# Turning raw input rows on TensorE and applying the RMS factor afterwards, in a hybrid decoder trunk

## The chip, the cores and the metric

The kernel runs on one core of a Trainium2 chip. The metric is the device time of one execution in microseconds (us), median of several runs. Before the change it is 637.72 us (3 runs, 635.66 to 637.82).

## The reference, cut to what matters

One inference step for 272 prompt rows (16 meta rows and 256) and 32 sample rows, 304 in all, of width 1024, in float32. Only its beginning is touched by the change:

```
xp = concatenate([meta, x_prompt])                 # 272 rows; x_sample gives 32 more
xn = x * rsqrt(mean(x * x, axis=-1) + EPS) * norm1_g
proj = xn @ w_in                                   # 1024 x 6144
u_x, u_y, c_v, c_g, g_rnn, g_conv = split(proj)
```

What follows: a gated recurrence on u_x (a convolution over 4 rows, block-diagonal gates, a linear scan), a convolution over 31 rows on c_v * sigmoid(c_g) with a layer norm, two projections, a gated merge, w_out and a residual, then a second RMS norm, a router that picks 2 of 32 experts for each row, the experts, and a last RMS norm.

## The kernel before, in words

Each engine has a program of its own, written out by hand in order; semaphores connect them. An engine does its instructions in that order, so an instruction that waits holds up all that stands behind it on the same engine.

**Layout.** The 304 rows arrive as three row tiles (`x[:, t]`, 128, 128 and 48 rows, rows on the partitions). The projections want channels on the partitions, so x is turned into `xnT`, eight column blocks of 128 channels by 304 rows. `w_in` comes in blocks of 512 columns (2 MB) through four slots of a buffer called `ring`. A tile of the projection is 128 output channels by 304 rows: eight matmuls into one PSUM bank (`bank[m % 4]`). The order of tiles is cv 0, cg 0, cv 1, cg 1 and so on, then ux, uy, gr, gc. After tile 2 TensorE turns the convolution's states (`conf_states`, line 1327).

**SyncE (lines 345 to 370)** issues x in five loads, the first half of weight block 0, nine small parameter loads of 4 KB (lines 355 and 357), then the weight blocks (line 367). Block 2 waits until all of x is turned, because the scaled rows `xn` lie in its slot; block 3 waits for the states' transposes.

**ScalarE (from line 530)** issues four larger parameter loads (the two convolutions' weights, two states), loads a function table, and squares the rows of x as they land, with a sum (line 550). It takes the root (line 553), later evicts every odd column block with the scale `norm1_g` (line 558), and then issues the convolution's state and the gates' weights (lines 560 to 568) before it comes to the projection's tiles.

**VectorE (from line 842)** finishes 1 / root (lines 854, 856), scales the rows (line 860), copies the turned parameters and states from PSUM (lines 863, 866), and evicts every even column block with `norm1_g` (line 871). Then it makes a few constants, copies the states (line 893), and goes on to the convolutions (lines 907, 910, 938).

**TensorE (from line 1312)** does 24 warm-up matmuls, waits for all 13 parameter loads (`par_in`), turns parameters (line 1319) and recurrence states (line 1322), waits for the scaled rows, turns them (line 1337, 8 column blocks of 3 transposes, through banks 4 to 7), waits for all evictions, and starts on tile 0 (line 1375).

Of the kernel before, what the change touches and what calls it, by code (L numbers as in the profile page):

```python
# [7 lines left out]
ALU = mybir.AluOpType  # L8
ACT = mybir.ActivationFunctionType
# [6 lines left out]
P = 128  # L16
HP = P // 2
D = 1024
KT = D // P
# [4 lines left out]
T = TP + NS * TS  # L24
ROWS = (P, P, T - 2 * P)
NT = len(ROWS)
# [23 lines left out]
BLOCK_WORDS = KT * WB  # L50
# [7 lines left out]
RESULTS_BEFORE = 2  # L58
ST_DMAS = 6 + NS
WO_BANKS = (0, 1, 2, 3, 6, 7)  # L60
TURN_BANKS = (4, 5, 4, 5, 4, 5, 3, 6)
EXP_WORDS = 2 * KT * F + FT * D

# [18 lines left out]
def trunk(nc, a, o):  # L82
    with ExitStack() as ctx:
# [3 lines left out]
        start = {}  # L87
# [12 lines left out]
        bank = [ctx.enter_context(nc.psum_tensor(f"bank{i}", [P, 512], F32))[:, :] for i in range(8)]  # L100


        ring = sb("ring", EXP_SLOTS * EXP_WORDS)
        x = sb("x", NT * D).rearrange("p (t d) -> p t d", t=NT)
        work = sb("work", WORK)
# [11 lines left out]
        def chan(ap):  # L117
# [4 lines left out]
        xnT = chan(cut(KT * T))  # L122
# [11 lines left out]
        at_glu, at_cc = KT * (T + UXN + HN), KT * (T + UXN + HN + GLN)  # L134
# [45 lines left out]
                for s in range(MIX_SLOTS)]  # L180
        w_hi = [rounded(f"w_hi{s}", "ring", e_hi + s * BLOCK_WORDS // 2, BLOCK_WORDS // 2) for s in range(HI_SLOTS)]

        xn = ring[:, 2 * BLOCK_WORDS:2 * BLOCK_WORDS + NT * D].rearrange("p (t d) -> p t d", t=NT)
        cut(0, 3 * BLOCK_WORDS)
        prow = cut(6 * P).rearrange("p (i n) -> p i n", i=6)
        crow = cut(16 * P).rearrange("p (i n) -> p i n", i=16)
# [21 lines left out]
        pn1, pccb, plg, plb, prcb, pba, pbi, plam = (par[:, i * KT:(i + 1) * KT] for i in range(8))  # L208
# [18 lines left out]
        ident, ones_d = sb("ident", P), sb("ones_d", P)  # L227
        tri, ones_b = sb("tri", P, BF16), sb("ones_b", P, BF16)
        lam = sb("lam", 5 * KT).rearrange("p (i c) -> p i c", i=5)
        stat, spare = sb("stat", 18), sb("spare", 1)  # L230


        (xhi_done, xlo_done, wlo_pool, par_in, first_in, cst_in, wbd_in, router_in, g_in, consts, zeros, dconst, dstep, astep, pstep, rstep,
         ss_done, ms_done, rs_done, xn_done, par_T, par_done, rst_T, rst_done, cst_T, cst_done, xT_done, xnT_done, xnT_act,
         lam_e, kappa_done, tile_mm, tile_act, tile_dve, glu_done, win_done, win_used, conv_done, xc_done,
         gate_mm, gate_act, dec_done, vsq_done, vrt_done, inp_done, scan_done, gelu_done, prod_done,
         st_cp, st_T, st_ev, st_out, mean_mm, cen_done, sq_done, sum_done, var_mm, var_done, std_done, nrm_done, silu_done,
# [3 lines left out]
         chi_done, clo_done, mhi_done, mlo_done, eg_mm, gu_mm, silu2, hid_done, dn_mm, ys_act, ys_dve,  # L241
         yT_mm, yT_act, yT_dve, y_mm, y_done, ss3_done, ms3_done, rs3_done, fin_done, y_out) = (sem(n) for n in (
            "xhi_done xlo_done wlo_pool par_in first_in cst_in wbd_in router_in g_in consts zeros dconst dstep astep pstep rstep "
            "ss_done ms_done rs_done xn_done par_T par_done rst_T rst_done cst_T cst_done xT_done xnT_done xnT_act "
            "lam_e kappa_done tile_mm tile_act tile_dve glu_done win_done win_used conv_done xc_done "
            "gate_mm gate_act dec_done vsq_done vrt_done inp_done scan_done gelu_done prod_done "
            "st_cp st_T st_ev st_out mean_mm cen_done sq_done sum_done var_mm var_done std_done nrm_done silu_done "
# [95 lines left out]
        def _(sp):  # L343
# [6 lines left out]

            sp.dma_start(mix_w[0][:, 0:HB], block_src(*blocks[0])[:, 0:HB]).then_inc(first_in, 16)

            for i, n in enumerate(("norm1_g", "conf_conv_b", "conf_ln_g", "conf_ln_b",
                                   "rnn_conv_b", "b_rg_a", "b_rg_i", "rg_lambda")):
                sp.dma_start(prow[i * KT:(i + 1) * KT, 0], a[n][0].rearrange("(c p) -> c p", p=P)).then_inc(par_in, 16)

            sp.dma_start(prow[64:64 + KT, 3], a["norm2_g"][0].rearrange("(c p) -> c p", p=P)).then_inc(par_in, 16)

            def load_block(b):
                if b == 2:  # L360
                    sp.wait_ge(xT_done, KT)
                if b == 3:
                    sp.wait_ge(cst_T, 4)
                if b >= MIX_SLOTS:
                    sp.wait_ge(*block_used(b - MIX_SLOTS))
                k = slice(HB if b == 0 else 0, KT)
                sp.dma_start(mix_w[b % MIX_SLOTS][:, k], block_src(*blocks[b])[:, k]).then_inc(mix_in[b % MIX_SLOTS], 16)
# [159 lines left out]
        @block.scalar  # L527
        def _(act):

            act.dma_start(prow[64:96, 0], a["rnn_conv_w"][0].rearrange("w (c p) -> (w c) p", p=P)).then_inc(par_in, 16)  # L530
            act.dma_start(prow[0:124, 1:3], a["conf_conv_w"][0].rearrange("w (c p) -> (w c) p", p=P)
                          .rearrange("(i r) p -> r i p", i=2)).then_inc(par_in, 16)
# [14 lines left out]
            act.wait_ge(dconst, 1)  # L547
            for t in range(NT):
                act.wait_ge(x_in[t], 16 if t == 1 else 32)
                nc.scalar.activation(xn[0:ROWS[t], t], x[0:ROWS[t], t], ACT.Square,  # L550
                                     accum_out=stat[0:ROWS[t], t:t + 1]).then_inc(ss_done, 1)
            act.wait_ge(ms_done, 1)
            nc.scalar.activation(stat[:, 3:6], stat[:, 3:6], ACT.Sqrt).then_inc(rs_done, 1)

            act.wait_ge(par_done, 1)
            for j in range(1, KT, 2):
                act.wait_ge(xT_done, j + 1)
                nc.scalar.activation(xnT[:, j], bank[4 + j % 4][:, 0:T], ACT.Copy, scale=pn1[:, j:j + 1]).then_inc(xnT_act, 1)  # L558

            act.dma_start(crow[0:120], a["state_conformer_conv"][0].rearrange("s r (c p) -> (s r c) p", p=P)  # L560
                          .rearrange("(i q) p -> q i p", i=16)).then_inc(cst_in, 16)
# [6 lines left out]
            act.dma_start(o["cc_s"][0][:, 0:CW - 1 - TS], a["state_conformer_conv"][0][:, TS:]).then_inc(st_out, 16)  # L568


            nc.scalar.activation(lam[:, 0], plam, ACT.Abs).then_inc(astep, 1)
            act.wait_ge(astep, 1)
            nc.scalar.activation(lam[:, 0], lam[:, 0], ACT.Exp, scale=-1.0).then_inc(lam_e, 1)
# [256 lines left out]
        def _(dve):  # L830
# [20 lines left out]
            def inverse_root(i, done, ms, rs):  # L851

                dve.wait_ge(done, NT)
                vec.tensor_scalar(stat[:, i + 3:i + 6], stat[:, i:i + 3], 1.0 / D, EPS, ALU.mult, ALU.add).then_inc(ms, 1)
                dve.wait_ge(rs, 1)
                step(vec.reciprocal(stat[:, i + 3:i + 6], stat[:, i + 3:i + 6]))

            inverse_root(0, ss_done, ms_done, rs_done)
            for t in range(NT):
                vec.tensor_scalar(xn[0:ROWS[t], t], x[0:ROWS[t], t], stat[0:ROWS[t], 3 + t:4 + t], None,  # L860
                                  ALU.mult).then_inc(xn_done, 1)
            dve.wait_ge(par_T, 1)
            vec.tensor_copy(par, bank[0][:, 0:416]).then_inc(par_done, 1)

            dve.wait_ge(rst_T, 1)
            vec.tensor_copy(state_cols(ux, UXP, UXS)[:, :, 0:RW - 1],
                            bank[1][:, 0:192].rearrange("p (s r c) -> p s r c", s=NS, r=RW - 1)).then_inc(rst_done, 1)
            dve.wait_ge(par_done, 1)
            for j in range(0, KT, 2):
                dve.wait_ge(xT_done, j + 1)  # L870
                vec.tensor_scalar(xnT[:, j], bank[4 + j % 4][:, 0:T], pn1[:, j:j + 1], None, ALU.mult).then_inc(xnT_done, 1)

            dve.wait_ge(lam_e, 1)
            e, z, z2, q = lam[:, 0], lam[:, 3], lam[:, 4], lam[:, 1]
# [431 lines left out]
        def _(pe):  # L1306
# [21 lines left out]
                ins.then_inc(cst_T, 1)  # L1328


            pe.wait_ge(xn_done, NT)
            for j in range(KT):
                if j >= 4:
                    pe.wait_ge(xnT_done if j % 2 == 0 else xnT_act, (j - 4) // 2 + 1)
                for t in range(NT):
                    n = ROWS[t]
                    ins = tp(bank[4 + j % 4][:, t * P:t * P + n], xn[0:n, t, j * P:(j + 1) * P], ident[0:n, 0:n])
                ins.then_inc(xT_done, 1)
            pe.wait_ge(par_done, 1)
            pe.wait_ge(rst_done, 1)  # L1340
            pe.wait_ge(xnT_done, KT // 2)
            pe.wait_ge(xnT_act, KT // 2)

            def tile(m):
                k, c = tiles[m]
                b = blocks.index((k, c // MB))
                if m == 0:
                    pe.wait_ge(first_in, 16)
                if c % MB == 0:
                    pe.wait_ge(mix_in[b % MIX_SLOTS], 16 * (b // MIX_SLOTS + 1))  # L1350
                if m >= 4:
                    if m - 4 < NACT:
                        pe.wait_ge(tile_act, m - 3)
                    else:
                        pe.wait_ge(tile_dve, m - 3 - NACT)
                if m >= first_tile:

                    u = (m - first_tile) // 2
                    pe.wait_ge(*low_ready(u))
                    _, lo, hi = split_halves(u)  # L1360
                    def rows(ap):
                        return [ap[:, i] for i in range(KT)]
                    x_hi, x_lo, ready = {"rp": (rows(gel_hi), rows(gel_lo), glo_done),
                                         "cp": (rows(cc_hi), rows(cc_lo), clo_done)}.get(k, (xn_hi, rows(xn_lo), xlo_done))
                    cols = slice((c % 2) * P, (c % 2 + 1) * P)
                    for i in range(KT):
                        if c == 0:
                            pe.wait_ge(ready, i + 1)
                        for j, (w, xp) in enumerate(((hi, x_hi), (hi, x_lo), (lo, x_hi))):
                            ins = mm(bank[m % 4][:, 0:T], w[:, i, cols], xp[i],  # L1370
                                     start=(i == 0 and j == 0), stop=(i == KT - 1 and j == 2))
                    ins.then_inc(tile_mm, 1)
                    return
                for i in range(KT):
                    ins = mm(bank[m % 4][:, 0:T], mix_w[b % MIX_SLOTS][:, i, (c % MB) * P:(c % MB + 1) * P], xnT[:, i],  # L1375
                             start=(i == 0), stop=(i == KT - 1))
                ins.then_inc(tile_mm, 1)
# [263 lines left out]
```

## Time and profile before

| | |
|---|---|
| median of 3 runs | 637.72 us |
| profiled execution | 638.57 us |
| its span, first to last instruction | 636.8 us |
| PE busy | 585.7 us (92%) |
| DVE busy | 346.8 us (54%) |
| ACT busy | 186.6 us (29%) |
| POOL busy | 84.5 us (13%) |

Engines: PE is TensorE's matmuls, PEld its weight loads, DVE VectorE, ACT ScalarE, POOL GpSimd, SP SyncE; SPq and ACTq are the issues of DMAs by these engines. L1375 is line 1375 of the kernel. A transpose stands in the trace as a MATMUL with `ident`. A float32 matmul of 304 or 128 columns stands as two MATMUL records. Queue q1 is SyncE's, q10 ScalarE's.

### The profile page before, as it was taken

What the parts mean: (1) busy time and instruction counts of PE and PEld (TensorE: products, weight loads), DVE (VectorE), ACT (ScalarE), POOL (GpSimd) and SP (SyncE); (2) the same over time, 40 slices, a digit from 0 to 9 for tenths busy, and PEclk for the clock granted to TensorE, in tenths of its full rate; (3) what the DMA queues carried; (4) which work ended last, traced back from release to release, by engine and by line L of the source; (5) the groups of instructions that cost most, each with busy time, mean ns of one, the idle gap of its engine ahead of it and who ended that gap; (6) DMA issues with size and microseconds to landing.
All of it is one profiled execution on the core that took longest, in us unless ns stands there. A gap on an engine that the chain in (4) does not pass through costs nothing.

```text
span 636.8 us, 18581 instructions
## 1 busy us (share of the span) xinstructions
PE 585.7 (92%) x8095; PEld 522.7 (82%) x8095; DVE 346.8 (54%) x693; ACT 186.6 (29%) x310; POOL 84.5 (13%) x97
## 2 busy tenths in 40 slices
PE   4999999969979799999998978999999999999793
PEld 4677777747779799999776978899999999989682
DVE  2139997789989999958417971112211122111135
ACT  3121111463493254555235320102112011120133
POOL 1011000124449650014100000000000000000000
PEclk9599999989989799999999889999999999999998
DMA  9793425330333333361307719999999999999202
GB/s 239 253 248 132 167 75 191 133 132 0 133 134 132 133 133 133 134 201 56 144 1 292 302 32 402 369 426 422 422 421 423 422 421 422 422 422 421 95 1 74
DMA packets 41768, 145.08 MB, mean 228 GB/s; under 512 B 6966, under 2 KB 10278, under 8 KB 29430
## 3 DMA queue, kind: packets, MB, share of 16 engines
q1 hardware_dynamic: 33440, 140.88, 56.8%
q10 hardware_dynamic: 8294, 3.73, 2.7%
q8 instruction: 23, 0.38, 0.2%
q14 instruction: 11, 0.09, 0.0%
HBM read 143.02 MB, written 2.43 MB: 228 GB/s over the span
## 4 chain that ended last, share of the span: by engine, by line
PE 41%; DVE 10%; DMA 8%; issue 3%; ACT 1%; DVEq 0%; ACTq 0%
PE bank L1552 18%; PE bank L1566 8%; DMA ring<-w_exp_up 8%; PE bank L1440 5%; PE bank L1370 4%; PE bank L1616 2%; DVE w_lo L976 1%; PE bank L1466 1%; PE bank L1600 1%; DVE conv L1019 1%; ACT work L823 1%; PE bank L1312 0%; DVE gel_lo L976 0%; DVE work L1050 0%; PE bank L1451 0%
## 5 line engine op out<-in xcount | busy, mean ns | idle before, releaser
L1552 PE MATMUL bank<-work,ring 128*64 128x80 f32 x4096 | 149.5, 234 | 7.7 <-DMA ring<-w_exp_up 3.5
L1552 PEld LDWEIGHTS bank<-work,ring 128*64 128x64 f32 x4096 | 146.3, 139 | 9.1 <-issue 8.2
L1375 PE MATMUL bank<-work,ring 128*128 128x304 f32 x512 | 136.3, 427 | 0.9 <-ACT work L558 0.9
L1375 PEld LDWEIGHTS bank<-work,ring 128*128 128x128 f32 x512 | 99.5, 195 | 36.2 <-issue 3.6
L907 DVE SCALAR_TENSOR_TENSOR bank<-work,par,bank 128x272 f32<-128x272 f32 x232 | 96.4, 498 | 0.0
L1228 DVE TENSOR_TENSOR windows<-bank,outst 128x160 f32<-128x160 f32 x32 | 10.4, 325 | 134.3 <-ACT outst L778 134.3
L1566 PE MATMUL bank<-windows,ring 128*64 128x80 f32 x2048 | 76.4, 233 | 1.4 <-issue 1.4
L1566 PEld LDWEIGHTS bank<-windows,ring 128*64 128x64 f32 x2048 | 73.9, 137 | 1.6 <-issue 1.6
L976 DVE TENSOR_TENSOR w_lo<-ring,w_hi 128x2048 fp32r<-128x2048 f32 x17 | 40.2, 2367 | 15.9 <-ACT w_hi L639 15.9
L778 ACT ACTIVATE outst<-bank 128x160 f32<-128x160 f32 x32 | 9.7, 305 | 130.5 <-PE bank L1552 130.5
L1370 PE MATMUL bank<-xn_hi,w_hi 128*128 128x304 f32 x128 | 40.8, 319 | 7.0 <-DVE w_lo L976 3.7
L639 ACT ACTIVATE w_hi<-ring 128x2048 fp32r<-128x2048 f32 x20 | 38.1, 1908 | 17.6 <-issue 6.9
L1235 DVE COPY work<-bank 128x320 f32 x32 | 15.7, 492 | 45.8 <-PE bank L1566 45.8
L1370 PE MATMUL bank<-xn_lo,w_hi 128*128 128x304 f32 x128 | 40.4, 316 | 0.0
L1370 PE MATMUL bank<-xn_hi,w_lo 128*128 128x304 f32 x128 | 40.1, 314 | 0.0
L471 POOL TENSOR_TENSOR windows<-work,par 128x248 f32<-128x248 f32 x32 | 30.4, 984 | 25.5 <-DVE work L919 25.5
L785 ACT ACTIVATE work<-bank 128x320 f32 x32 | 14.1, 440 | 64.5 <-PE bank L1566 64.5
L1370 PEld LDWEIGHTS bank<-xn_hi,w_hi 128*128 128x128 f32 x128 | 25.6, 200 | 7.7 <-issue 7.7
L1312 PE MATMUL bank<-ident 128*128 128x128 f32 x144 | 22.3, 327 | 5.6 <-issue 4.1
L1312 PEld LDWEIGHTS bank<-ident 128*128 128x128 f32 x144 | 21.4, 239 | 5.9 <-issue 4.2
L1370 PEld LDWEIGHTS bank<-xn_lo,w_hi 128*128 128x128 f32 x128 | 25.8, 202 | 0.0
L1370 PEld LDWEIGHTS bank<-xn_hi,w_lo 128*128 128x128 f32 x128 | 25.7, 201 | 0.0
(273 smaller groups left out, 794.2 us busy)
## 6 DMA issues: line engine op xcount, KB each, us to landing
ring<-w_exp_gate SPq DMA_DIRECT2D x32, 1024.0 KB, 14.8
ring<-w_exp_up SPq DMA_DIRECT2D x32, 1024.0 KB, 15.3
ring<-w_exp_down SPq DMA_DIRECT2D x32, 1024.0 KB, 16.2
ring<-w_in SPq DMA_DIRECT2D x11, 2048.0 KB, 8.6
ring<-w_rnn_proj SPq DMA_DIRECT2D x2, 2048.0 KB, 7.9
ring<-w_conv_proj SPq DMA_DIRECT2D x2, 2048.0 KB, 8.3
ring<-w_out SPq DMA_DIRECT2D x2, 2048.0 KB, 8.3
ring<-w_in SPq DMA_DIRECT2D x2, 1024.0 KB, 10.9
```

The lines of the kernel that those rows point to most:

```text
L471: ins = nc.gpsimd.tensor_tensor(win4[:, :, t, :], g[:, :, t:t + CW], pcw[:, :, c].unsqueeze(1).broadcast_to([P, NS, CW]), ALU.mult)
L639: nc.scalar.activation(hi, w, ACT.Copy).then_inc(whi_done, 1)
L785: nc.scalar.activation(ys[:, 0:4, bass.ds(at, C)], bank[2 + 2 * b][:, 0:4 * C].rearrange("p (m n) -> p m n", m=4), ACT.Copy).then_inc(ys_a ...
L907: ins = vec.scalar_tensor_tensor(y, glu[:, ch, w:w + TP], pcw[:, w, ch:ch + 1], acc, ALU.mult, ALU.add)
L976: vec.tensor_tensor(part, value, as_f32(high), ALU.subtract).then_inc(lo_sem, 1)
L1235: vec.tensor_copy(ys[:, 4:8, bass.ds(at, C)], bank[3 + 2 * b][:, 0:4 * C].rearrange("p (m n) -> p m n", m=4)).then_inc(ys_dve, 1)
L1312: mm(bank[q][:, 0:P], ident, ident, start=True, stop=True)
L1370: ins = mm(bank[m % 4][:, 0:T], w[:, i, cols], xp[i], start=(i == 0 and j == 0), stop=(i == KT - 1 and j == 2))
L1375: ins = mm(bank[m % 4][:, 0:T], mix_w[b % MIX_SLOTS][:, i, (c % MB) * P:(c % MB + 1) * P], xnT[:, i], start=(i == 0), stop=(i == KT - 1))
L1440: ins = mm(bank[q][0:ROWS[t]], xp[:, c, tok], w[:, i], start=(c == 0 and j == 0), stop=(c == KT - 1 and j == 2))
L1552: ins = mm(bank[b][lo:lo + HP, (2 * m + f) * C:(2 * m + f + 1) * C], w_gu[s][m][:, k, f, lo:lo + HP], xw[b][:, k], start=(k == 0), stop=(k ...
L1566: ins = mm(bank[2 + 2 * b + m // 4][lo:lo + HP, (m % 4) * C:(m % 4 + 1) * C], w_dn[s][:, f, m * P + lo:m * P + lo + HP], hid[b][:, f], sta ...
```

## The change

The rows of x are turned as they are, without the factor 1 / root; the factor is applied to the turned blocks. For that the factors, which lie one to a partition, are spread along a row: three matmuls of a matrix of 1 / D with diagonal matrices (`diag`, the factors times D on the identity) give a bank in which every partition holds all 304 factors; ScalarE copies it to `inv_row`. VectorE evicts all eight column blocks, each with `norm1_g` and `inv_row` in one instruction; ScalarE evicts none of them.

TensorE turns seven column blocks for row tile 0, then for row tile 1, then for row tile 2, each into a bank of its own (`X_BANKS`); the eighth block uses the first one's bank again and is turned inside tile 0, after its first matmul. Tile 0 waits for the column blocks one by one.

VectorE copies the turned parameters and states before it computes the factors. The scaled rows are gone; the squares, `inv_row` and `diag` lie in a part of `work` that is not used until later, and weight block 2 no longer waits for the transposes. The nine small parameter loads are issued by ScalarE, ahead of its own four.

```diff
+X_BANKS = (2, 3, 4, 5, 6, 7, 1, 2)
...
@@ SyncE
-            for i, n in enumerate(("norm1_g", "conf_conv_b", "conf_ln_g", "conf_ln_b",
-                                   "rnn_conv_b", "b_rg_a", "b_rg_i", "rg_lambda")):
-                sp.dma_start(prow[i * KT:(i + 1) * KT, 0], a[n][0].rearrange("(c p) -> c p", p=P)).then_inc(par_in, 16)
-
-            sp.dma_start(prow[64:64 + KT, 3], a["norm2_g"][0].rearrange("(c p) -> c p", p=P)).then_inc(par_in, 16)
...
-                if b == 2:
-                    sp.wait_ge(xT_done, KT)
@@ ScalarE
+            for i, n in enumerate(("norm1_g", "conf_conv_b", "conf_ln_g", "conf_ln_b",
+                                   "rnn_conv_b", "b_rg_a", "b_rg_i", "rg_lambda")):
+                act.dma_start(prow[i * KT:(i + 1) * KT, 0], a[n][0].rearrange("(c p) -> c p", p=P)).then_inc(par_in, 16)
+            act.dma_start(prow[64:64 + KT, 3], a["norm2_g"][0].rearrange("(c p) -> c p", p=P)).then_inc(par_in, 16)
             act.dma_start(prow[64:96, 0], a["rnn_conv_w"][0].rearrange("w (c p) -> (w c) p", p=P)).then_inc(par_in, 16)
...
-            act.wait_ge(par_done, 1)
-            for j in range(1, KT, 2):
-                act.wait_ge(xT_done, j + 1)
-                nc.scalar.activation(xnT[:, j], bank[4 + j % 4][:, 0:T], ACT.Copy, scale=pn1[:, j:j + 1]).then_inc(xnT_act, 1)
+            act.wait_ge(inv_mm, 1)
+            nc.scalar.activation(inv_row, bank[0][:, 0:T], ACT.Copy).then_inc(inv_done, 1)
@@ VectorE
-            inverse_root(0, ss_done, ms_done, rs_done)
-            for t in range(NT):
-                vec.tensor_scalar(xn[0:ROWS[t], t], x[0:ROWS[t], t], stat[0:ROWS[t], 3 + t:4 + t], None,
-                                  ALU.mult).then_inc(xn_done, 1)
             dve.wait_ge(par_T, 1)
             vec.tensor_copy(par, bank[0][:, 0:416]).then_inc(par_done, 1)
...
+            inverse_root(0, ss_done, ms_done, rs_done)
+            dve.wait_ge(consts, 1)
+            for t in range(NT):
+                n = ROWS[t]
+                vec.tensor_scalar(diag[0:n, t, 0:n], ident[0:n, 0:n], stat[0:n, 3 + t:4 + t], float(D),
+                                  ALU.mult, ALU.mult).then_inc(diag_done, 1)
             dve.wait_ge(par_done, 1)
-            for j in range(0, KT, 2):
-                dve.wait_ge(xT_done, j + 1)
-                vec.tensor_scalar(xnT[:, j], bank[4 + j % 4][:, 0:T], pn1[:, j:j + 1], None, ALU.mult).then_inc(xnT_done, 1)
+            dve.wait_ge(inv_done, 1)
+            for c in range(KT):
+                dve.wait_ge(xT_done, c + 1)
+                vec.scalar_tensor_tensor(xnT[:, c], bank[X_BANKS[c]][:, 0:T], pn1[:, c:c + 1], inv_row,
+                                         ALU.mult, ALU.mult).then_inc(xnT_done, 1)
@@ TensorE
-            pe.wait_ge(xn_done, NT)
-            for j in range(KT):
-                if j >= 4:
-                    pe.wait_ge(xnT_done if j % 2 == 0 else xnT_act, (j - 4) // 2 + 1)
-                for t in range(NT):
-                    n = ROWS[t]
-                    ins = tp(bank[4 + j % 4][:, t * P:t * P + n], xn[0:n, t, j * P:(j + 1) * P], ident[0:n, 0:n])
-                ins.then_inc(xT_done, 1)
+            def turn_x(c, t):
+
+                n = ROWS[t]
+                ins = tp(bank[X_BANKS[c]][:, t * P:t * P + n], x[0:n, t, c * P:(c + 1) * P], ident[0:n, 0:n])
+                if t == NT - 1:
+                    ins.then_inc(xT_done, 1)
+
+            for t in range(NT):
+                pe.wait_ge(x_in[t], 16 if t == 1 else 32)
+                for c in range(KT - 1):
+                    if t == 0 and c == KT - 2:
+                        pe.wait_ge(rst_done, 1)
+                    turn_x(c, t)
             pe.wait_ge(par_done, 1)
-            pe.wait_ge(rst_done, 1)
-            pe.wait_ge(xnT_done, KT // 2)
-            pe.wait_ge(xnT_act, KT // 2)
+            pe.wait_ge(dconst, 1)
+            for t in range(NT):
+                n = ROWS[t]
+                pe.wait_ge(diag_done, t + 1)
+                ins = mm(bank[0][:, t * P:t * P + n], ones_d[0:n], diag[0:n, t, 0:n], start=True, stop=True)
+            ins.then_inc(inv_mm, 1)
+            pe.wait_ge(inv_done, 1)
...
                 for i in range(KT):
+                    if m == 0:
+                        pe.wait_ge(xnT_done, i + 1)
+                    if m == 0 and i == 1:
+                        for t in range(NT):
+                            turn_x(KT - 1, t)
                     ins = mm(bank[m % 4][:, 0:T], mix_w[b % MIX_SLOTS][:, i, (c % MB) * P:(c % MB + 1) * P], xnT[:, i],
```

## Rows read from the trace of the kernel before

**Rows 1.** The page's busy tenths of PE in 40 equal slices of the span.
```profile
PE   4999999969979799999998978999999999999793
```

**Rows 2.** PE's longest wait of the whole span: us in total, times, longest.
```profile
PE bank L1319 <- DMA ring<-norm_g: 6.6, 1, 6.6
```

**Rows 3.** Timeline: start us, us, engine, line, operation, count [idle before <-releaser].
```profile
15.93 0.96 PE L1319 MATMUL bank<-ident,ring 96*128 96x96 f32 x4 [6.62 <-DMA ring<-norm_g]
...
17.00 7.11 PE L1337 MATMUL bank<-ident,ring 128*128 128x128 f32 x24
...
17.56 0.56 PEld L1337 LDWEIGHTS bank<-ident,ring 48*128 48x128 f32 x3 [0.33 <-issue]
...
25.03 14.94 PE L1375 MATMUL bank<-work,ring 128*128 128x304 f32 x48 [0.92 <-ACT work L558]
```

**Rows 4.** Windows with PE's granted clock (after busy), and the timeline's weight loads.
```profile
22.00:24.00 2.00, 2.00 (x8) 0.50 0.05 20
...
...
30.00:32.00 2.00, 2.00 (x9) 1.00 1.08 340
...
25.67 0.34 PEld L1375 LDWEIGHTS bank<-work,ring 128*128 128x128 f32 x1 [0.17 <-issue]
...
29.73 9.76 PEld L1375 LDWEIGHTS bank<-work,ring 128*128 128x128 f32 x38 [0.17 <-issue]
```

**Rows 5.** Timeline of DVE: the first convolution, and the recurrence's second one.
```profile
47.36 1.03 DVE L910 TENSOR_SCALAR bank<-work,par 128x272 f32<-128x272 f32 x2 [0.65 <-POOL work L452]
...
103.58 0.45 DVE L938 TENSOR_SCALAR outst<-work,par 128x328 f32<-128x328 f32 x1 [3.54 <-ACT work L587]
```

**Rows 6.** Timeline of DMA issues: ACT's first and fourth, SP's block and small loads.
```profile
0.78 0.44 ACTq L530 DMA_DIRECT2D ring<-rnn_conv_w  x1
...
2.50 0.60 ACTq L534 DMA_DIRECT2D ring<-state_rglru_conv  x1
...
3.25 0.48 SPq L351 DMA_DIRECT2D ring<-w_in  x1
3.77 0.45 SPq L355 DMA_DIRECT2D ring<-norm_g  x1
...
6.61 0.30 SPq L357 DMA_DIRECT2D ring<-norm_g  x1
```

**Rows 7.** DMA queues (packets, MB, share): 0:4 twice, 0:14, 10:12, 22:24; block 1's landing.
```profile
q1 hardware_dynamic: 118, 0.41, 38.7%
q10 hardware_dynamic: 228, 0.11, 10.1%
...
q10 hardware_dynamic: 588, 0.27, 11.4%
...
q10 hardware_dynamic: 34, 0.02, 5.0%
...
q1 hardware_dynamic: 24, 0.04, 5.4%
...
ring<-w_in SPq DMA_DIRECT2D x1, 2048.0 KB, 15.7
```

**Rows 8.** Timeline rows that give the price of an operation.
```profile
13.35 2.07 DVE L860 TENSOR_SCALAR ring<-x,stat 128x1024 f32<-128x1024 f32 x3
...
17.43 0.48 DVE L866 COPY work<-bank 128x192 f32<-128x192 f32 x1
...
40.16 0.41 ACT L582 ACTIVATE ring<-bank 128x304 f32<-128x304 f32 x1
...
103.95 0.55 DVE L940 SCALAR_TENSOR_TENSOR conv<-work,par,conv 128x328 f32<-128x328 f32 x1
...
349.75 5.91 PE L1312 MATMUL bank<-ident 128*128 128x128 f32 x36
```

**Rows 9.** Timeline of ACT: issues of the gates' weights, and its first work behind them.
```profile
24.60 8.41 ACTq L565 DMA_DIRECT2D gate_weights<-w_rg_a  x2
...
38.52 0.21 ACT L571 ACTIVATE lam<-par 128x8 f32<-128x8 f32 x1 [13.87 <-issue]
```

More of the change, by code:

```diff
@@ L181, in trunk @@
         w_hi = [rounded(f"w_hi{s}", "ring", e_hi + s * BLOCK_WORDS // 2, BLOCK_WORDS // 2) for s in range(HI_SLOTS)]
-        xn = ring[:, 2 * BLOCK_WORDS:2 * BLOCK_WORDS + NT * D].rearrange("p (t d) -> p t d", t=NT)
+        x_sq = work[:, at_cc:at_cc + NT * D].rearrange("p (t d) -> p t d", t=NT)
+        inv_row = work[:, at_cc + NT * D:at_cc + NT * D + T]
+        diag = work[:, at_cc + NT * D + T:at_cc + NT * D + T + NT * P].rearrange("p (t n) -> p t n", t=NT)
         cut(0, 3 * BLOCK_WORDS)
@@ L233, in trunk @@
         (xhi_done, xlo_done, wlo_pool, par_in, first_in, cst_in, wbd_in, router_in, g_in, consts, zeros, dconst, dstep, astep, pstep, rstep,
-         ss_done, ms_done, rs_done, xn_done, par_T, par_done, rst_T, rst_done, cst_T, cst_done, xT_done, xnT_done, xnT_act,
+         ss_done, ms_done, rs_done, diag_done, inv_mm, inv_done, par_T, par_done, rst_T, rst_done, cst_T, cst_done, xT_done, xnT_done,
          lam_e, kappa_done, tile_mm, tile_act, tile_dve, glu_done, win_done, win_used, conv_done, xc_done,
@@ L243, in trunk @@
             "xhi_done xlo_done wlo_pool par_in first_in cst_in wbd_in router_in g_in consts zeros dconst dstep astep pstep rstep "
-            "ss_done ms_done rs_done xn_done par_T par_done rst_T rst_done cst_T cst_done xT_done xnT_done xnT_act "
+            "ss_done ms_done rs_done diag_done inv_mm inv_done par_T par_done rst_T rst_done cst_T cst_done xT_done xnT_done "
             "lam_e kappa_done tile_mm tile_act tile_dve glu_done win_done win_used conv_done xc_done "
@@ L549, in _ @@
                 act.wait_ge(x_in[t], 16 if t == 1 else 32)
-                nc.scalar.activation(xn[0:ROWS[t], t], x[0:ROWS[t], t], ACT.Square,
+                nc.scalar.activation(x_sq[0:ROWS[t], t], x[0:ROWS[t], t], ACT.Square,
                                      accum_out=stat[0:ROWS[t], t:t + 1]).then_inc(ss_done, 1)
@@ L568, in _ @@
             act.dma_start(o["cc_s"][0][:, 0:CW - 1 - TS], a["state_conformer_conv"][0][:, TS:]).then_inc(st_out, 16)
+            act.wait_ge(par_done, 1)
             nc.scalar.activation(lam[:, 0], plam, ACT.Abs).then_inc(astep, 1)
```

## The prediction
> **What bounds the kernel now.** First the busy line in 40 slices: PE is at nine tenths or more in most of them, so what moves the dense start of PE's work moves the end, unless another engine or the DMAs take over in between [rows 1]. Then PE's waits over the whole span: the longest one is 6.6 us, and it stands in the part that is changed [rows 2]. PE has done its warm-up matmuls by 9.3 us and then waits until 15.92 for the last of the 13 parameter loads (norm_g on SP's queue). Call this moment T0. The timeline shows the rest of the opening [rows 3]: at 15.93 six transposes of parameters and states, from 17.00 the 24 transposes of the scaled rows (7.11 us), at 25.03 the first matmul of tile 0. So tile 0 starts at T0 + 9.1.
>
> From there on PE runs without a wait. The granted clock is 0.50 (1.2 GHz) during the transposes and until shortly before 30, then 1.00 (2.4 GHz). In the slow part one weight load plus its gap takes 0.34 + 0.17 = 0.51 us, and 38 of them take 9.76 us, 0.26 each, in the fast part [rows 4]; a matmul of 304 columns is two such records, so 1.02 us slow and 0.51 us fast.
>
> Does an earlier tile 0 reach the end? VectorE's convolution starts at 47.36 after a wait of 0.65 us for tile 3's result, and at 103.58 it waits another 3.54 us for ScalarE's copy of a PE result [rows 5]. Both follow PE, so a shift of tile 0 passes on to the following stages one for one, within the 3.5 us by which VectorE may be late. The weights of the later blocks are requested when PE frees a slot, so they move along too.
>
> **The change part by part.** The new order on PE is: T0, six parameter transposes, 21 transposes of raw rows, three matmuls with diagonals, then tile 0. PE does not look at x before the parameters are there, because its program has the parameter transposes first. So the first question is T0.
>
> *When the parameters land.* SP issued the nine small loads from 3.77 to 6.91, behind x and half of block 0. Now ScalarE's queue takes them ahead of its own four loads. SP's pace was 0.33 us each (3.14 us for nine); while both queues were issuing, one of SP's took 0.48. So the four loads, issued from 0.78 to 3.10 before, come 3.0 to 4.3 us later, ending at 6.1 to 7.4 [rows 6]. These four then become the last: before, their queue (q10) moved 588 packets, 228 of them by 4 us while SP's queue had moved only 118, and it still had 34 packets between 10 and 12; I put the last at 11.5, which is 8.4 us after the last issue [rows 7]. With the same 8.4 us the last packet comes at 14.5 to 15.8. But the easy first 228 are gone: by the time the four are issued, SP's queue is full of x and weights. The other 360 packets went at 360 / 7.5 us = 48 a us; all 588 at that pace take 12.3 us, from 4.9 to 6.4 (1.2 us after the issue starts, as before) to 17.2 to 18.7. For landing I add 0.6: block 1, issued at about 7.3 (one issue after SP's small ones end), landed 15.7 us later, at 23.0, with its queue's last 24 packets between 22 and 24 [rows 7]. So T0 is 15.1 to 16.4 by the one, 17.8 to 19.3 by the other. I take 16.8, nearer to the first, which is the same four loads measured whole: 0.9 us later than before.
>
> Of the Trainium skill one rule bears on this: DMA: Bandwidth & Descriptors, "Why a DMA increments its semaphore by 16 and not by 1", says that a load runs on the largest number of engines up to 16 that divides its outer dimension. conf_conv_w has 124 rows, so four engines would carry all 248 pieces; the count of 588 fits that (536 pieces and 16 + 4 + 16 + 16 completions). By an estimate from it the tail of the four loads is a matter of these four engines and not of the queue's rate, and moving other loads about does not shorten it; spread over 16 engines, T0 would be nearer to 13.
>
> *The path from T0 to tile 0.*
> - Parameter and state transposes, unchanged: 15.92 to 17.00, 1.1 us.
> - 21 transposes instead of 24. Before, one cost 7.11 / 24 = 0.30 us, with a gap of 0.33 ahead of each 48-row one [rows 3]. The new order does all 128-row ones first, so six of seven gaps go: 21 x 0.30 - 6 x 0.33 = 4.2 us. The ends are 6.2 (no gap goes) and 3.8 (the six parameter transposes took 0.18 each).
> - Three fp32 matmuls of a diagonal. 36 records of 128 columns took 5.91 us, partly at the low clock [rows 8]; two records each: 6 x 0.16 = 1.0 us. The ends are 0.5 and 1.3 (128/304 of 1.02, three times).
> - ScalarE's copy of the row, 0.41, and VectorE's first product, 0.55 (row of 328 elements) [rows 8]. Each hand-over costs what the old one did: 0.92 us of idle PE for a copy of 0.51 [rows 3], so 0.4 each. Together 1.8 us; ends 1.2 and 2.2.
> - Sum: 1.1 + 4.2 + 1.0 + 1.8 = 8.1, so tile 0 starts at T0 + 8.1, 1.0 us nearer than before. The remaining seven products (about 0.5 us each) stay ahead of matmuls of 1.02 us, and later of 0.51 just about.
> - The eighth column block is turned inside tile 0, three transposes: 7.11 / 8 = 0.9 us (ends 0.5 and 0.9).
> The path is worth -1.0 + 0.9 = -0.1 us, with T0 +0.9: **tile 0's work is 0.8 us later**. A part of it runs at the low clock in both kernels; if the clock rises at the same moment, half of the delay is all that is lost. I take +0.5.
>
> *Edits that I cost at nothing.* Scaling x on VectorE (2.07 us [rows 8]) goes; it ran in the wait for parameters. The two copies from PSUM come before the inverse root now and end at T0 + 2.0 (17.91 before [rows 8]); root and three diagonals follow, even at the old 2.07 us for the three done by about T0 + 4.8, under the transposes, which end at T0 + 5.3. If those took 3.8, the diagonals would be as late as the transposes, no more. ScalarE's nine issues end by 7.4, and its table load (1.28) and the squares then start about 1 us late; they are wanted only at T0 + 2.0. The half of block 0 and block 1 leave SP 3 us earlier, into a queue that is busy anyway. Block 2 no longer waits for the transposes; PE needs it only after tile 7, over 30 us later. Its 2 MB then no longer run beside ScalarE's state load, whose issues held ScalarE from 24.60 to 38.5 [rows 9]; that frees ScalarE earlier, but PE did not wait for ScalarE there, so it gives nothing.
>
> **Sum.** The profiled execution took 638.57 us (span 636.8): 638.57 + 0.5 = 639.1. It lies 0.85 above the median of the runs, 637.72, so by the median 638.2.
>
> **The rivals.**
> 1. *The parameters do land early.* If the tail of ScalarE's loads shortens once x is in, and they finish at the pace of their first 4 us, T0 comes at about 12.5: -3.4 - 0.1 = -3.5 us, 634.2. For it: 228 packets in the first 2 us of transfers [rows 7]. Against it: those met a nearly empty queue beside them. The state load's issue moves with T0, so it would not take the gain away.
> 2. *Slower: the four loads crawl against the weight stream.* All 588 packets at 48 a us and issued at the slow pace, T0 = 19.3: +3.4 - 0.1 = +3.3, and 641.0. It decides against the kernel as soon as T0 is later than about 16.0, and beyond the measurement from 19.2. For it: block 2's 2 MB now stand right behind block 1 in SP's queue. Against it: x is out of the way sooner.
> 3. *The clock rises during the denser transposes.* It would save half of 2 us of transposes, 0.5 on the diagonals, 0.4 on the eighth block and 2.4 of the 4.8 us that tile 0 spent at half clock [rows 3, 4]: -4.3 + 0.8 = -3.5, 634.2. Against it: 8 us of transposes left it at 0.50 [rows 4].
>
> **How the numbers follow.** Forecast 0.62, rival 1 0.15, rival 2 0.15, rival 3 0.08. 0.5% is 3.2 us, about what a measurement of this kernel can tell from no change. Rivals 1 and 3 lie at that edge, so some 0.17 of their 0.23 lies beyond, and 0.01 of the forecast: faster 0.18. Of rival 2, 0.1 and of the forecast 0.02: slower 0.12. The rest, 0.70, is no change. The range goes from rival 1 to rival 2, 634.3 to 641.1; the forecast's own is 636.5 to 640.
>
> **What would show it.** The first parameter transpose in the trace gives T0 (16.8; rival 1 under 14; rival 2 over 18.5), and the loads on which it waited must be ScalarE's, not SP's. The row transposes should take about 4.2 us, tile 0 start at T0 + 8.1, its first two matmuls lie 0.9 us apart, and the clock be 0.50 until tile 0 is well under way. VectorE's convolution should start within 1 us of 47.4. A T0 more than 3 us off would make the prediction wrong; a clock of 1.00 before tile 0 would too.

## The result: 645.26 us, and the profile after

The changed kernel took 645.26 us (median of 4 runs, 642.01 to 647.71), the kernel before 637.77 beside it (4 runs, 635.66 to 639.16): a ratio of 1.010, 95% interval 1.007 to 1.013. The forecast was 638.2 and no change; the time lies above the range. The profiled execution took 646.54 us, its span is 644.8.

PE's busy line of the page after. Against [rows 1] two slices fall from 9 to 6: the second, in the opening, and the thirteenth, from 193 to 209 us.

```profile
PE   4699999969976898999999889899999999999793
```

PE's longest wait (us in total, times, longest) is the same one as in [rows 2], but 4.2 us longer and for a load of ScalarE's queue.

```profile
PE bank L1321 <- DMA ring<-state_rglru_conv: 10.8, 1, 10.8
```

The timeline of the opening (columns as in [rows 3]): six parameter transposes, 21 of rows, the diagonals, ScalarE's copy, VectorE's products, tile 0 with the eighth block inside it.

```profile
19.84 0.96 PE L1321 MATMUL bank<-ident,ring 96*128 96x96 f32 x4 [10.81 <-DMA ring<-state_rglru_conv]
...
20.90 4.10 PE L1336 MATMUL bank<-ident,x 128*128 128x128 f32 x21
24.94 1.81 PE L1351 MATMUL bank<-work,ones_d 128*128 128x128 f32 x6
26.78 0.42 ACT L555 ACTIVATE work<-bank 128x304 f32<-128x304 f32 x1 [4.71 <-PE bank L1351]
27.30 3.63 DVE L872 SCALAR_TENSOR_TENSOR work<-bank,par,work 128x304 f32<-128x304 f32 x8 [4.34 <-ACT work L555]
27.98 1.35 PE L1391 MATMUL bank<-work,ring 128*128 128x304 f32 x2 [1.23 <-DVE work L872]
29.12 0.90 PE L1336 MATMUL bank<-ident,x 128*128 128x128 f32 x3
```

T0 is 19.84, where [rows 3] has 15.93. From T0 to tile 0 it is 8.14 us, where it was 9.1. So tile 0 starts 2.95 us later (27.98 against 25.03), and the eighth block inside it (0.90) makes its work 3.85 us late. Of that, 3.38 us arrive at VectorE's first convolution, which starts at 50.74 [rows 5: 47.36].

```profile
50.74 1.03 DVE L912 TENSOR_SCALAR bank<-work,par 128x272 f32<-128x272 f32 x2 [4.33 <-POOL work L447]
```

PE's windows (stretch, length, PE busy and records, granted clock, DMA share, GB/s), the first from the kernel before and the other two from after. A mean of 0.52 puts the rise from 0.50 to 1.00 near 29.9, a mean of 0.81 near 32.8: an estimate from these means. So the clock rises 2.8 us later where the work is 3.85 us later: about 1 us less of it is spent at 0.50, and half of that is the difference to 3.38.

```profile
28.00:30.00 2.00, 2.00 (x5) 0.52 1.04 343
...
30.00:32.00 2.00, 2.00 (x5) 0.50 1.17 216
32.00:34.00 2.00, 2.00 (x8) 0.81 1.26 162
```

ScalarE's issues [rows 6]: the nine small loads from 0.78, the four large ones behind them from 4.20.

```profile
4.20 0.37 ACTq L529 DMA_DIRECT2D ring<-rnn_conv_w  x1
...
5.62 0.90 ACTq L533 DMA_DIRECT2D ring<-state_rglru_conv  x1
```

Packets of ScalarE's queue q10 (packets, MB, share of 16 engines) in the stretches 0:4, 0:10, 10:12 and 12:20. In [rows 7] the queue had moved 228 by 4 us.

```profile
q10 hardware_dynamic: 38, 0.01, 1.1%
q10 hardware_dynamic: 222, 0.07, 3.3%
q10 hardware_dynamic: 267, 0.13, 24.2%
q10 hardware_dynamic: 243, 0.12, 5.4%
```

Together the last three are 732, which is 588 and nine times 16 for the small loads. Taken in the order of issue, their 144 and the first 78 of the large ones are all that the queue moves in ten microseconds. Then 267 come in two, and the last 243 take eight more. Both ends of that are in T0: a late start and a long tail.

**The other 5 us.** The span is 8.0 us longer, and the opening gives 3.4. The rest comes between 190 and 220 us, where VectorE and GpSimd both have work on SBUF. VectorE after (start, us, operation): its weight subtraction (w_lo), the step on the windows (L924), the scan's next part, and the channel sum.

```profile
193.68 9.22 DVE L978 TENSOR_TENSOR w_lo<-ring,w_hi 128x2048 fp32r<-128x2048 f32 x1
...
205.67 0.93 DVE L924 TENSOR_SCALAR work<-work,par 128x32 f32<-128x32 f32 x1
...
213.44 0.24 DVE L924 TENSOR_SCALAR work<-work,par 128x32 f32<-128x32 f32 x1
...
214.41 6.19 DVE L978 TENSOR_TENSOR w_lo<-ring,w_hi 128x2048 fp32r<-128x2048 f32 x1
...
248.48 4.47 DVE L1021 TENSOR_REDUCE conv<-work 128x304 f32<-128x2432 f32 x1
```

The same instructions of VectorE before:

```profile
190.33 2.62 DVE L976 TENSOR_TENSOR w_lo<-ring,w_hi 128x2048 fp32r<-128x2048 f32 x1
...
195.71 3.82 DVE L922 TENSOR_SCALAR work<-work,par 128x32 f32<-128x32 f32 x1
...
206.38 2.10 DVE L922 TENSOR_SCALAR work<-work,par 128x32 f32<-128x32 f32 x1
...
209.22 2.97 DVE L976 TENSOR_TENSOR w_lo<-ring,w_hi 128x2048 fp32r<-128x2048 f32 x1
...
240.02 4.66 DVE L1019 TENSOR_REDUCE conv<-work 128x304 f32<-128x2432 f32 x1
```

The two subtractions are 6.60 and 3.22 us longer, the two steps on the windows 2.89 and 1.86 shorter: 3.71 + 1.36 = 5.07. From the first convolution to the channel sum it is 197.74 us after and 192.66 before, 5.08 more. So nothing else in these 190 us adds to the time. From the channel sum to the end it is 0.5 us less than before.

GpSimd at that moment, after: products back to back, then its own 4.56 us subtraction, to 200.75.

```profile
193.37 0.78 POOL L489 TENSOR_TENSOR work<-work 128x272 f32<-128x272 f32 x1
...
196.19 4.56 POOL L496 TENSOR_TENSOR w_lo<-ring,w_hi 128x2048 fp32r<-128x2048 f32 x1
```

And before:

```profile
190.00 0.80 POOL L494 TENSOR_TENSOR work<-work 128x272 f32<-128x272 f32 x1
190.74 2.31 POOL L495 TENSOR_TENSOR work<-work 128x32 f32<-128x32 f32 x1
```

In both, VectorE comes 0.3 us into a product of GpSimd's. Before, it gets in at that product's end, and GpSimd's small one stands for 2.31 us, the length of a subtraction. After, it stands from 193.68 until GpSimd has ended at 200.75, and needs 2.15 from there. The two engines meet at the same relative time; who goes first differs. Call this the meeting; VectorE loses it when it is the one that stands. There are ten profiles of the kernels of this document, those of experiments 8 and 9 aside. In all of them VectorE comes 0.30 to 0.34 us into a product. It goes first in seven (2.60 to 2.62 us) and loses in three (9.22 or 9.23: this one and those of experiments 6 and 7). So the moment of arrival doesn't decide it, and what does was not found.

By the Trainium skill, SBUF — State Buffer, "Who interferes with whom", the two share a pair of ports under an exclusive lock, and the one that gets it keeps the other out. The traces agree: before, GpSimd's small product stands for one subtraction of VectorE's; after, VectorE stands for 7.07 us, through the rest of GpSimd's products and its subtraction.

### The profile page after: what moved, and what is told of

Its sections match the earlier page's. It is cut to its first block, busy times and chain, and to the rows that moved or that the text cites. A ratio compares the mean times of both kernels' runs of the same rounds, so it can differ in the third digit from the quotient of the medians.

```text
span 644.8 us, 18594 instructions
## 1 busy us (share of the span) xinstructions
PE 588.0 (91%) x8101; PEld 528.6 (82%) x8101; DVE 351.7 (55%) x697; ACT 184.9 (29%) x307; POOL 84.5 (13%) x97
## 4 chain that ended last, share of the span: by engine, by line
PE 45%; DMA 7%; DVE 7%; issue 2%; ACT 1%; DVEq 0%; ACTq 0%
PE bank L1568 18%; PE bank L1582 8%; PE bank L1381 8%; DMA ring<-w_exp_up 7%; PE bank L1456 5%; PE bank L1632 2%; PE bank L1482 1%; PE bank L1616 1%; DVE conv L1021 1%; PE bank L1314 1%; ACT work L821 1%; DVE gel_lo L978 0%; PE bank L1467 0%; DVE x L1303 0%; DVE work L1193 0%
## 5 line engine op out<-in xcount | busy, mean ns | idle before, releaser
L978 DVE TENSOR_TENSOR w_lo<-ring,w_hi 128x2048 fp32r<-128x2048 f32 x17 | 50.1, 2950 | 15.8 <-ACT w_hi L637 15.8
L1381 PE MATMUL bank<-xn_hi,w_hi 128*128 128x304 f32 x128 | 40.4, 316 | 10.3 <-DVE w_lo L978 7.0
## 6 DMA issues: line engine op xcount, KB each, us to landing
ring<-w_exp_down SPq DMA_DIRECT2D x32, 1024.0 KB, 15.1
```

What stands on the lines that cost most here:

```text
L978: vec.tensor_tensor(part, value, as_f32(high), ALU.subtract).then_inc(lo_sem, 1)
L1381: ins = mm(bank[m % 4][:, 0:T], w[:, i, cols], xp[i], start=(i == 0 and j == 0), stop=(i == KT - 1 and j == 2))
```

## Experiments

Theory A: T0 is late because ScalarE's large loads queue behind nine small ones that make little way beside SP's x and weights, and the transposing front by itself is no loss. Rival B: the new front, or block 2 now standing in SP's queue early, is what costs.

**1. Changed kernel, the nine small loads back on SP.**
```diff
+            sp.dma_start(prow[i * KT:(i + 1) * KT, 0], a[n][0]...)  # nine, behind x and half of block 0
-            act.dma_start(prow[i * KT:(i + 1) * KT, 0], a[n][0]...)
```


> The changed kernel, but the nine small parameter loads are again issued by SyncE, where they were. Theory A (the nine loads ahead of ScalarE's four made the last of these land late): T0, PE's first parameter transpose, is back at 15.5 to 16.5 us; the path T0 to tile 0 stays 8.1, so tile 0 starts at about 24.1; the first convolution on VectorE starts at 47.0 to 47.6 (before 47.36, after 50.74), and the time is that of before, 636 to 640 us. Theory B (the new order of transposes, diagonals and evictions costs the time): T0 returns too, but the time stays at 643 to 647.

Measured 638.46 (10 runs; before 639.66 beside it), ratio 0.999 [0.996, 1.002]. PE's timeline, its window 20 to 22, and VectorE's first convolution:

```profile
16.13 0.96 PE L1323 MATMUL bank<-ident,ring 96*128 96x96 f32 x4 [6.87 <-DMA ring<-norm_g]
...
17.20 3.42 PE L1338 MATMUL bank<-ident,x 128*128 128x128 f32 x21
20.55 1.06 PE L1353 MATMUL bank<-work,ones_d 128*128 128x128 f32 x6
22.84 1.21 PE L1393 MATMUL bank<-work,ring 128*128 128x304 f32 x2 [1.23 <-DVE work L874]
```
```profile
20.00:22.00 2.00, 1.61 (x14) 1.00 1.05 387
```
```profile
44.94 1.03 DVE L914 TENSOR_SCALAR bank<-work,par 128x272 f32<-128x272 f32 x2 [1.65 <-POOL work L453]
```

T0 is back, and tile 0 comes 2.2 us earlier than before. The path is 6.71 and not the 8.1 expected, and the convolution comes at 44.94, ahead of the 47.0 to 47.6 expected, because the clock rose during the transposes. So in the opening the front saves more than was forecast, and the queue move is the loss. Block 2 is asked for without a wait here as in the changed kernel: it is not the cause. The median moves by less than its interval, so a gain of the front in time is not shown; the profiled execution (636.89) is the third fastest of the ten.

**2. Kernel before, only the loads moved.** The same nine loads taken from SP and put ahead of ScalarE's four.
```diff
-            sp.dma_start(prow[i * KT:(i + 1) * KT, 0], a[n][0]...)
+            act.dma_start(prow[i * KT:(i + 1) * KT, 0], a[n][0]...)  # nine, ahead of the four
```


> The kernel before, with the nine small loads moved to ScalarE's queue ahead of its own four, and nothing else of the change. Theory A: T0 19 to 21 us, tile 0 at T0 + 9.1 = 28 to 30, convolution at 51 to 52, time 641 to 646 us, as slow as the whole change or slower. Theory B: the time of before, 636 to 639.

Measured 643.64 (5 runs; before 639.66, for experiments 3 and 4 too), ratio 1.0056 [1.0025, 1.0087].

```profile
20.06 0.95 PE L1317 MATMUL bank<-ident,ring 96*128 96x96 f32 x4 [10.20 <-DMA ring<-state_rglru_conv]
...
29.16 15.16 PE L1373 MATMUL bank<-work,ring 128*128 128x304 f32 x48 [0.92 <-ACT work L556]
```

With the old front T0 is 20.06 and the path still 9.1: the move alone costs the 4 us of T0, and the kernel is slower. A holds, B falls.

**3. Changed kernel, the four large loads first.**
```diff
             act.dma_start(prow[64:96, 0], a["rnn_conv_w"]...)  # and the other three
+            act.dma_start(prow[i * KT:(i + 1) * KT, 0], a[n][0]...)  # nine
```


> The changed kernel, with ScalarE's own four loads issued first and the nine small ones behind them. Theory A: the four are done by about 11.5 us as before and the small ones a little later, T0 12.5 to 14.5; tile 0 at T0 + 8.1 = 21 to 22.5, convolution at 44 to 46, time 634 to 637 us. Rival C (thirteen loads on ScalarE's queue are late in any order, because its queue gets too small a share beside the weights): T0 18 to 20, time 641 to 647.

Measured 636.85 (7 runs), ratio 0.9946 [0.9924, 0.9968]. PE's wait, and q10's packets in 0:4 and 12:16:

```profile
PE bank L1321 <- DMA ring<-norm_g: 6.4, 1, 6.4
```
```profile
q10 hardware_dynamic: 181, 0.08, 7.5%
q10 hardware_dynamic: 96, 0.03, 3.1%
```

The large loads start early again (181 packets by 4 us, against 38). T0 is 15.83: 4.0 earlier than in the changed kernel, but not as early as expected, since the small loads are now the slow tail, 96 packets in four microseconds, and the last to land is one of them. The convolution starts at 44.98, as expected. Rival C falls: the order in the queue counts. The nine loads of 4 KB are slow on this queue behind the large ones as well as ahead of them.

**4. Changed kernel, conf_conv_w in two loads.**
```diff
-            act.dma_start(prow[0:124, 1:3], ...)
+            for lo, hi in ((0, 112), (112, 124)):
+                act.dma_start(prow[lo:hi, 1:3], ...[lo:hi])
```


> The changed kernel, with the load of conf_conv_w (124 partitions) issued as two, of 112 and of 12 partitions. If its 124 partitions put it on four DMA engines, as the Trainium skill's page on DMA says in its section on how many engines a load uses, the long tail on ScalarE's queue goes: T0 13 to 15, convolution 44.5 to 46.5, 634 to 638 us. If the tail is the queue's rate beside the weights, T0 stays at 19 to 20.5 and the time at 642 to 647.

Measured 637.20 (10 runs), ratio 0.9962 [0.9932, 0.9992]. q10's packets in 10:12, 12:14 and 14:16, and PE's start:

```profile
q10 hardware_dynamic: 272, 0.13, 24.3%
q10 hardware_dynamic: 289, 0.13, 24.9%
q10 hardware_dynamic: 17, 0.00, 1.0%
```
```profile
15.06 0.95 PE L1322 MATMUL bank<-ident,ring 96*128 96x96 f32 x4 [5.34 <-DMA ring<-state_rglru_conv]
```

The start is as late as in the changed kernel (272 packets in 10:12, 267 there). The tail is gone: what took eight microseconds takes two, and T0 is 4.8 earlier. So the two halves of the fault are separate, and either repair takes T0 to 15 or 16. The four engines that the Trainium skill gives to 124 rows (DMA: Bandwidth & Descriptors, "Why a DMA increments its semaphore by 16 and not by 1") agree with this tail. The prediction's estimate from it, T0 near 13, missed by two, for the late start.

**5. The changed kernel again, 12 runs.**

> The changed kernel once more, unchanged. T0 should be late again, 19 to 21 us, and the first convolution at 50 to 52. Theory D: the rest of its 644.8 us span (4 us more between the convolution and the sum over channels than in any other profile) is chance, two VectorE subtractions of 2.3 us that stood behind GpSimd for 9.2 and 6.2 us; then this profile has them at 2.3 to 3.0, the distance from convolution to channel sum is 192.5 (197.7 in the first profile), and the median over more runs is 641 to 644. Rival: the change itself causes them; then they are long again and the median is 645 or more.

Measured 642.48 (639.99 to 646.49; before 640.79 in 29 runs), ratio 1.0046 [1.0012, 1.008]. VectorE's first convolution, its subtraction and its channel sum in this profile:

```profile
49.66 1.03 DVE L912 TENSOR_SCALAR bank<-work,par 128x272 f32<-128x272 f32 x2 [4.33 <-POOL work L447]
...
192.62 2.62 DVE L978 TENSOR_TENSOR w_lo<-ring,w_hi 128x2048 fp32r<-128x2048 f32 x1
...
242.07 4.61 DVE L1021 TENSOR_REDUCE conv<-work 128x304 f32<-128x2432 f32 x1
```

T0 is 20.82, tile 0 27.56 (the clock rose in the transposes, as in experiment 1), the first convolution 49.66 (just ahead of the 50 to 52 expected) and the channel sum 242.07: from the one to the other 192.41 us, as before. The same program that lost the meeting in its first profile wins it here, and its span is 638.6 instead of 644.8. Against the kernel before that is 1.8 more: 2.3 at the first convolution, and nothing added behind it. This belongs to the change. The other 5 us are there in one execution of the same program and not in another.

**6. The loads as early as they can be.** Changed kernel, the nine small ones on SP ahead of block 0, and conf_conv_w split as in 4.
```diff
+            sp.dma_start(prow[i * KT:(i + 1) * KT, 0], a[n][0]...)  # nine, behind x
             sp.dma_start(mix_w[0][:, 0:HB], block_src(*blocks[0])[:, 0:HB]).then_inc(first_in, 16)
```


> The changed kernel with the nine small loads issued by SyncE between x and the first half of block 0, and conf_conv_w in two loads (112 and 12 partitions). Theory A (T0 is what counts, and small loads are quick on a queue that has nothing beside them but ScalarE's four): T0 11.5 to 13.5, tile 0 at T0 + 7 to 8 = 19 to 21, convolution at 41.5 to 44, time 632 to 636 us. Rival C (small loads are slow wherever they stand beside a second busy queue): T0 15 to 16, 636 to 639.

Measured 634.33 (12 runs, 631.6 to 638.96), ratio 0.9897 [0.9864, 0.993] to the 29 runs of before in experiment 5, as in experiment 7: faster than both kernels. The profiled execution is its slowest run, 638.96; PE's timeline and VectorE's subtraction show both sides.

```profile
10.32 0.58 PE L1324 MATMUL bank<-ident,ring 96*128 96x96 f32 x4 [1.77 <-DMA ring<-norm_g]
...
17.82 1.35 PE L1394 MATMUL bank<-work,ring 128*128 128x304 f32 x2 [1.23 <-DVE work L875]
```
```profile
183.01 9.23 DVE L981 TENSOR_TENSOR w_lo<-ring,w_hi 128x2048 fp32r<-128x2048 f32 x1
```

T0 (10.32), tile 0 (17.82) and the convolution (40.15) all come earlier than expected, and rival C falls. Tile 0 is 7.2 us earlier than before. This execution lost the meeting (9.23), and that eats most of it.

**7. The same two repairs in the kernel before.**

> The kernel before, with the nine small loads between x and block 0's first half on SyncE and conf_conv_w in two loads, and nothing else. Theory A: T0 11.5 to 13.5, but the scaled rows are ready only at about 15.4, so PE turns them from 15.5 and tile 0 starts at 23.3 to 23.8, convolution at 45.5 to 46.5, time 635.5 to 638. If T0 alone set tile 0 (9.1 us behind it), it would start at 21 to 22.5 and the time be 633 to 636.

Measured 635.99 (10 runs), ratio 0.9936 [0.9896, 0.9975]. VectorE's subtraction:

```profile
186.47 9.22 DVE L977 TENSOR_TENSOR w_lo<-ring,w_hi 128x2048 fp32r<-128x2048 f32 x1
```

T0 is 10.59 and tile 0 at 20.87. PE does wait for the scaled rows, but only 1.45 us (until 12.78), so tile 0 lies below both ranges expected. This profile, of the slowest of the ten runs (642.33), lost the meeting with the old front: the new one is not needed for that. Parameters landing early are the larger part of the gain, without the new front. The front adds three microseconds to tile 0 (20.87 to 17.82) and 1.7 us to the medians, with intervals that overlap, so that this last gain is not shown.

**8 and 9. Holding GpSimd back.** Can the meeting be taken away? GpSimd's products wait for VectorE's third subtraction, in the changed kernel and in kernel 6 (that of experiment 6).
```diff
             pool.wait_ge(gelu_done, 1)
+            pool.wait_ge(wlo_done, 3)
```


> The changed kernel, with GpSimd's products (which start while VectorE has a weight subtraction to do) held until that subtraction is done. Theory D (when the two engines meet there, it is chance which waits, and a VectorE that loses stands 6 to 7 us behind GpSimd's back-to-back instructions): that subtraction takes 2.3 us, convolution to channel sum is 192 to 195 in every case, T0 stays at 19 to 21, and the spread between the runs falls; median 640 to 643, no run above 645. Rival: the spread comes from elsewhere, and runs of 645 to 647 remain.

> par_early with the same hold on GpSimd. Theory D: its profile with a lost meeting had 637.2 us of span and a channel sum at 237.75, 197.6 after the convolution; with the hold that distance is 192 to 195, the runs lie between 631 and 634.5, the median at 632 to 633.5 (par_early 634.3). Rival (the hold only moves the meeting to GpSimd's next instructions, or delays the products that PE needs): median 634 or more.

Measured 647.82 (4 runs, 646.45 to 648.80), ratio 1.0127 [1.0069, 1.0185], and 639.92 (12 runs), ratio 1.001 [0.9975, 1.0046] (before 639.28, for experiment 10 too). Both are outside what theory D expected. VectorE in the second:

```profile
201.81 1.19 DVE L925 TENSOR_REDUCE work<-windows 128x32 f32<-128x992 f32 x1 [6.75 <-POOL windows L472]
203.03 6.55 DVE L928 TENSOR_SCALAR work<-work,par 128x32 f32<-128x32 f32 x1
```

The subtraction is short now (2.28 and 2.29), and the next instructions pay: VectorE waits 6.75 us for GpSimd's windows, then a step that takes 0.24 in the changed kernel stands for 6.55 beside GpSimd's next subtraction and its next products. From the convolution to the channel sum it is 199.4 us in both, more than the 197.74 of a lost meeting. The hold moves the loss to the next instructions; it is no remedy.

**10. Rows first.** Kernel 6 with six column blocks turned ahead of the parameters, the seventh behind the diagonals, and the parameter copies behind the inverse roots.
```diff
+                for c in range(KT - 2):  # for each token tile, ahead of the wait for parameters
+                    turn_x(c, t)
             pe.wait_ge(par_in, 16 * 14)
```


> par_early, with six column blocks of x turned ahead of the parameters, the seventh behind the diagonals while PE waits for ScalarE and VectorE, the eighth inside tile 0, and the factors made ahead of the parameter copies. Tile 0 waits for the landing of block 0 at about 15.7 (par_early 17.82), and only one block is turned inside it, so its work is 1.5 to 2.1 us ahead of par_early's: convolution at 38.3 to 39.5, if the clock rises as in par_early; median 631 to 634. If the state load's landing (needed after tile 2, at 31 to 32) is the next bound, the convolution stays at 39.5 to 40.2, and there is no gain over par_early.

Measured 634.35 (8 runs, 632.79 to 635.98), ratio 0.9904 [0.9871, 0.9937]: no gain over kernel 6.

```profile
15.44 0.75 PE L1395 MATMUL bank<-work,ring 128*128 128x304 f32 x2 [1.34 <-DMA ring<-w_in]
...
32.79 2.65 PE L1323 MATMUL bank<-ident,ring 120*128 120x120 f32 x16 [2.30 <-DMA ring<-state_conformer_conv]
```

Tile 0 starts 2.4 us sooner, bound by block 0's landing, and PE later waits 2.30 us for a state load. The convolution starts at 42.06, 1.9 us later than in kernel 6 and beyond both ranges expected. By this one profile, loads bound the opening in this order of issue.

(An earlier form of this, with block 6 inside tile 0 too, computes something else in part of its outputs, and its time is not used.)

## Why the prediction was wrong, step by step

- **"When the parameters land": the step that failed.** Forecast T0 16.8, with ends at 15.1 and 19.3; measured 19.84, beyond both. The issues came as forecast: the nine took 3.42 us, and the four ended at 6.52, within 6.1 to 7.4 (though 3.14 us for nine is 0.35 each, not 0.33). What failed is the time from issue to landing. The two prices were fit to the four loads as they ran alone in their queue, and I started them 1.2 us after their issue. Experiments 1 to 4 show what took the place of that: most of their packets move only from 10 us on, when the nine ahead of them are through, and the last 243 crawl as long as conf_conv_w is one load. [Rows 7] had the sign of it: 228 packets by 4 us were a head start that the move gave away. I wrote that down and then took the end that assumes it kept. With the 3.4 us that the opening lost the sum gives 642.0 for the profiled execution; the other 4.5 of the 646.54 belong to the step on the shift, below. By the prediction's own sign, a T0 more than 3 us off, it is wrong (3.04).
- **Rival 2 had the size, not the cause.** It gave T0 19.3 and +3.3 for the opening (measured 19.84 and +3.4), and named block 2 in SP's queue. Experiment 1 has block 2 early and T0 16.13; experiment 2 has it late and T0 20.06.
- **Rival 1** did not happen with the loads where the change puts them. Where they are issued ahead of the weights, T0 is 10.3 (experiment 6) and the gain is more than it gave.
- **The path of 8.1 us: right** (8.14). The transposes took 4.10, forecast 4.2, and the eighth block 0.90 as forecast. Inside the sum two terms were off and cancel: the diagonals took 1.81 and not 1.0, which is what they take at the full clock (1.06 where the clock is 1.00, experiment 1), and the copy with its hand-overs 1.23 and not 1.8.
- **"Half of the delay is all that is lost": wrong.** It takes the clock to rise at the same moment. The clock rose 2.8 us later, and of the 3.85 us by which tile 0's work was late 3.38 arrive at the convolution.
- **Rival 3** did not happen in the profile of the changed kernel, but it is real: in experiment 1 the granted clock is 1.00 in the window 20 to 22 with only transposes and diagonals on PE since 16.13, and the path is 6.71. In experiment 5 the path is 6.74. "8 us of transposes left it at 0.50" was one execution. What it gave is 1.4 us of path and, at the convolution, 2.1 to 2.7 us against what was expected; in time no gain is shown (experiment 1).
- **A shift of tile 0 passes on one for one: right as far as 190 us, and the second step that failed.** What I had not seen is that VectorE and GpSimd meet there, at 5 us a time: 5.08 of the profiled execution's 8.0 us. The opening alone takes 637.72 to 641.1, the upper end of the range; only with the lost meeting does the profiled execution lie well beyond it. That it was lost in the profiled execution was chance as far as the profiles tell. The row was in the trace of before, a 128x32 product of GpSimd's at 2.31 us among others of 0.25. I had read no further than the second convolution.
- **Bounds of 0.5%.** By experiment 5 the change costs 0.46%, 2.9 us (interval 0.1 to 0.8%); the medians there differ by 1.7. The 1.0% of the first four runs may contain more executions that lost the meeting, but one of the four was profiled; how often a kernel loses it, and whether the change makes that more frequent, was not settled. The kernel before spreads too: 635.84 to 646.18 in 29 runs.

One reading of a row was off without consequence: the issues in [rows 9] that held ScalarE are those of the gates' weights, not of the state load.

Left open: whether the nine small loads are slow by their number or by SP's traffic beside them. No run had them alone.

## What to carry to other kernels

Here loads that were put ahead of others in a queue made those late (T0 19.84 against 15.83 with the order turned round). Before loads are moved to a queue, look at what stands behind them, and price those from the moment the newcomers are through, not from their own issue. Count the packets of a queue in short windows; a late start and a long tail have different remedies (the order of the loads, the shape of one load), and here either gave back 4 to 5 us of T0. And where two engines share a resource, look in the old trace for one instruction that takes many times its siblings' time: that can be a meeting, and another execution of the same program may have the other engine wait, at another price.

## What was not expected of the hardware

- One VectorE subtraction of 2.28 us took 9.22 with the operands unchanged, standing behind several instructions of GpSimd's and not one; the same program took 2.62 in another execution.
- With nine loads of 4 KB at its head a queue moved 222 packets in the first ten microseconds and 267 in the next two; with the large loads ahead of them it had moved 181 by 4 us, against 38.
- One load of 124 rows, split into 112 and 12, brought the end of 13 loads from 19.84 to 15.06.
- PE's granted clock during the 21 transposes of one program stayed at 0.50 in one execution and rose in another (experiment 5), with durations of 4.10 and 3.45 us.
